# A two-layer fp32 decoder on one core: which engine makes the low halves of forty weight tiles

## The reference, cut to what matters

```python
def self_decoder_layer(x, mem, ...):
    proj = rmsnorm(x, norm_attn) @ w_in
    o_sb = stick_breaking_attention(...)
    o_mem = memory_branch(q_mem, mem, norm_mem, w_mem_kv)
    x = x + jnp.concatenate([o_sb.reshape(...), o_mem], axis=-1) @ w_out
    return x + conv_ffn(rmsnorm(x, norm_ffn), ffn_up, ffn_conv, ffn_down)
...
for g, (window, dilation) in enumerate(DIL_GROUPS):
    o_g, lse_g = dilated_window_attention(q_dil[:, :, hs], k_sh[:, :, hs], v_sh[:, :, hs], slopes[hs], window, dilation)
alpha = jax.nn.softmax(jnp.stack(lses, axis=0), axis=0)
```

## Time and profile before

| | |
|---|---|
| median of 3 runs | 1273.68 us (1272.54 to 1274.01) |
| profiled execution | 1273.02 us, of which the span from first to last instruction is 1271.2 |
| TensorE (PE) busy | 1217.4 us, 96% of the span |
| VectorE (DVE) busy | 800.3 us, 63% |
| ScalarE (ACT) busy | 553.7 us, 44% |
| GpSimd (POOL) busy | 102.6 us, 8% |
| granted TensorE clock, mean | 0.995 of full |

### The profile page before, as it was taken

The page is one execution under the profiler, slowest core; times in us unless marked ns, Lnnn a source line. Parts: engine busy times, 40 slices in busy tenths (PEclk is TensorE's granted clock), DMA queues, the critical chain, the costliest instruction groups (busy, mean ns, idle before and its releaser), DMA issues.

```text
span 1271.2 us, 16965 instructions
## 1 busy us (share of the span) xinstructions
PE 1217.4 (96%) x5975; PEld 999.4 (79%) x5975; DVE 800.3 (63%) x1243; ACT 553.7 (44%) x918; POOL 102.6 (8%) x133
## 2 busy tenths in 40 slices
PE   4889999989999999999999999889999999999998
PEld 3777888868788888878887877778788888888886
DVE  4956666664677777762247776776777777774226
ACT  4535666653444444441235553534544444442222
POOL 0301333333000000000002000000200000000000
PEclk9989999999999999999999999999999999999999
DMA  7411211203233333322251122121333333333552
GB/s 222 129 50 50 68 50 51 67 1 112 88 100 99 92 91 97 99 98 99 88 163 32 52 68 82 51 67 57 93 96 90 96 99 99 95 95 104 140 138 74
DMA packets 179796, 112.50 MB, mean 88 GB/s; under 512 B 20062, under 2 KB 171934, under 8 KB 179742
## 3 DMA queue, kind: packets, MB, share of 16 engines
q1 hardware_dynamic: 179742, 111.79, 29.6%
HBM read 107.58 MB, written 2.10 MB: 86 GB/s over the span
## 4 chain that ended last, share of the span: by engine, by line
PE 83%; DVE 10%; ACT 3%; issue 2%; DMA 1%; POOL 0%; DVEq 0%; SPq 0%; ACTq 0%; POOLq 0%
PE bank L1334 17%; PE bank L1336 17%; PE bank L1335 16%; PE bank L1614 8%; PE bank L1641 8%; DVE w_lo L881 2%; PE bank L1627 2%; PE bank L1561 2%; PE bank L1654 1%; DVE y_lo L887 1%; PE bank L1486 1%; PE bank L1488 1%; PE bank L1487 1%; PE bank L1539 1%; ACT w_hi L582 1%
## 5 line engine op out<-in xcount | busy, mean ns | idle before, releaser
L1334 PE MATMUL bank<-y_hi,w_hi 128*128 128x512 f32 x928 | 366.9, 395 | 3.7 <-DVE w_lo L881 2.6
L1336 PE MATMUL bank<-y_hi,w_lo 128*128 128x512 f32 x928 | 362.3, 390 | 0.0
L1335 PE MATMUL bank<-y_lo,w_hi 128*128 128x512 f32 x928 | 362.2, 390 | 0.0
L881 DVE TENSOR_TENSOR w_lo<-raw,w_hi 128x1024 fp32r<-128x1024 f32 x188 | 230.7, 1227 | 162.5 <-ACT w_hi L582 159.8
L582 ACT ACTIVATE w_hi<-raw 128x1024 fp32r<-128x1024 f32 x186 | 196.3, 1056 | 305.7 <-PE bank L1336 146.3
L1334 PEld LDWEIGHTS bank<-y_hi,w_hi 128*128 128x128 f32 x928 | 174.9, 188 | 43.0 <-issue 4.9
L1336 PEld LDWEIGHTS bank<-y_hi,w_lo 128*128 128x128 f32 x928 | 174.7, 188 | 37.0
L1335 PEld LDWEIGHTS bank<-y_lo,w_hi 128*128 128x128 f32 x928 | 175.0, 189 | 36.6 <-issue 1.2
L1614 PE MATMUL bank<-ar,w_hi 128*128 (+1 forms) x288 | 88.8, 390 | 0.8 <-DVE af L1099 0.8
L741 ACT ACTIVATE af<-af,conv 128x512 f32<-128x512 f32 x88 | 63.0, 716 | 37.0 <-DVE af L1099 37.0
L1641 PE MATMUL bank<-w_hi,ar 128*128 128x512 f32 x288 | 77.1, 390 | 0.8 <-DVE af L1099 0.8
(11 more groups left out here) (200 smaller groups left out, 1613.5 us busy)
## 6 DMA issues: line engine op xcount, KB each, us to landing
raw<-in_a_ffn_up SPq DMA_DIRECT2D x44, 512.0 KB, 3.7
raw<-in_b_ffn_up SPq DMA_DIRECT2D x44, 512.0 KB, 3.7
raw<-in_a_ffn_down SPq DMA_DIRECT2D x22, 512.0 KB, 3.2
raw<-in_b_ffn_down SPq DMA_DIRECT2D x22, 512.0 KB, 3.6
raw<-in_a_w_in SPq DMA_DIRECT2D x20, 512.0 KB, 3.8
raw<-in_w_kv_shared SPq DMA_DIRECT2D x12, 512.0 KB, 3.8
raw<-in_a_w_out SPq DMA_DIRECT2D x8, 512.0 KB, 3.7
raw<-in_b_w_in SPq DMA_DIRECT2D x8, 512.0 KB, 3.8
```

Of the source, the lines that this page charges most:

```text
L881: nc.vector.tensor_tensor(w_lo[:, m % SPLIT, :], raw[:, m % RAW, :], w_hi[:, m % SPLIT, :].bitcast(F32), ALU.subtract).then_inc(lo_done, 1)
L1334: mm(bank, w[0], y[0][:, k, :], start=(k == 0), stop=False)
L1335: mm(bank, w[0], y[1][:, k, :], start=False, stop=False)
L1336: last = mm(bank, w[1], y[0][:, k, :], start=False, stop=(k == KT - 1))
```

## The change

The low halves of forty tiles are made by GpSimd in place of VectorE: `POOL_LOW` holds the numbers 30 to 39 and 104 to 133. The instruction is the same tensor_tensor subtraction on 128x1024. GpSimd waits for `hi_done` and for `lo_done` of the tile before, so that the count stays in order. `squares` becomes `square(e, k)`, so that low halves can stand between the eight sums. In the output projection of layer A each of the eight low halves stands ahead of one sum, and two more (for the first pair of the up projection) follow; in layer B two stand ahead of the attention, 18 and then 8 follow the order of `SEQ_B`, and two come at the end. VectorE's `ring` returns for these tiles, without the wait for `hi_done`; ahead of the loop over the up projection's tiles VectorE waits until `lo_done` has reached the first tile that it makes again. GpSimd calls `ring` at some places for tiles that are not in `POOL_LOW`, and nothing happens there.

```diff
+        POOL_LOW = set(itertools.chain(range(N_OUTA + 2, N_UPA + 4), range(N_QMB + 2, N_UPB + 4)))
...
         @block.gpsimd
         def _(pool):
-            def squares(e):
...
+            def ring(n):
+
+                if n in POOL_LOW:
+                    pool.wait_ge(hi_done, n + 1)
+                    pool.wait_ge(lo_done, n)
+                    nc.gpsimd.tensor_tensor(w_lo[:, n % SPLIT, :], raw[:, n % RAW, :], w_hi[:, n % SPLIT, :].bitcast(F32),
+                                            ALU.subtract).then_inc(lo_done, 1)
+
+            def square(e, k):
...
-            squares(1)
-            squares(2)
-            squares(3)
+            for k in range(KT):
+                ring(N_OUTA + k + 2)
+                square(1, k)
+            ring(N_UPA + 2)
+            ring(N_UPA + 3)
+            for k in range(KT):
+                square(2, k)
+            ring(N_QMB + 2)
+            ring(N_QMB + 3)
+            for op, *a in SEQ_B:
+                if op == "P" and a[3] == KT:
+                    ring(nb(a[0], a[1]) + 2)
+                if op == "O":
+                    u, x = divmod(a[0], KT)
+                    if a[1] == OUT_KS_B[u][-1]:
+                        if x % 2:
+                            ring(N_OUTB + a[0] // 2 + 2)
+                        if u:
+                            square(3, x)
+            ring(N_UPB + 2)
+            ring(N_UPB + 3)
...
             def ring(n, m=None):
 
                 m = n if m is None else m
+                if isinstance(n, int):
+                    if n in POOL_LOW:
+                        return
+                    if n - 1 in POOL_LOW:
+                        dve.wait_ge(lo_done, n)
                 dve.wait_ge(hi_done, n + 1)
...
+                if n_up + 3 in POOL_LOW:
+                    dve.wait_ge(lo_done, n_up + 4)
                 with dve.Fori(0, 7) as i:
```

More of the change, by code:

```diff
@@ L11 @@
+import itertools
 from contextlib import ExitStack
@@ L511, in _ @@
         def _(pool):
-            def squares(e):
[L514 to L524, removed]
-                    else:
-                        ins = nc.gpsimd.tensor_tensor(ss[:], ss[:], sq[:, k % 2, :], ALU.add)
-                    ins.then_inc(ss_add, 1)
-            nc.gpsimd.memset(vv_gap.bitcast(F32), 0.0).then_inc(vv_zero, 1)
-            squares(0)
+            def ring(n):
[5 more added lines that the diff above has]
+            def square(e, k):
+                c = 8 * e + k
+                pool.wait_ge(sq_done, c + 1)
+                if c:
+                    pool.wait_ge(ss_add, c)
+                if k == 0:
+                    if e == 0:
+                        pool.wait_ge(tab_tr, 1)
+                    else:
+                        pool.wait_ge(ss_done, e)
+                    ins = nc.gpsimd.tensor_copy(ss[:], sq[:, 0, :])
+                else:
+                    ins = nc.gpsimd.tensor_tensor(ss[:], ss[:], sq[:, k % 2, :], ALU.add)
+                ins.then_inc(ss_add, 1)
+            nc.gpsimd.memset(vv_gap.bitcast(F32), 0.0).then_inc(vv_zero, 1)
+            for k in range(KT):
+                ring(k + 2)
+                square(0, k)
+            for n in range(N_QMA + 2, N_ATA + 5):
+                ring(n)
             added = 0
```

## The result

The changed kernel takes 1300.45 us in the median (1297.10 to 1304.07) against 1273.11 for the kernel before in the same runs: 1.0213 times as long, 95% interval 1.0193 to 1.0233, 27.3 us more. The prediction said 1287 with a range to 1296. The side was right, but the 13.3 us forecast are half of the 27.3 measured. The profiled execution took 1303.25 us, its span 1301.4.

The account below looks back on a forecast made before the run. The prediction took TensorE to bound the kernel, so only added TensorE waits count. Its eight terms summed to 13.3 us, taking the median from 1273.68 to 1287.0 us, with a range of 1277 to 1296.

Parts of the forecast that it names:

- the term: Start of the up projections: L898 and the eviction stand behind GpSimd's low half, +1.0 us in A and +1.0 in B.
- term 4: Attention, second score block: late softmax and tensor_scalar L1204 blocked by GpSimd, +2.3 us; 0.4 if not blocked.
- 5 first half: Coefficients of the first three heads: small chain behind a late qk_low, transposes behind a blocked L1247, +1.4 us.
- term 6: Attention tile at 806.01 whose low half TensorE itself already waits for, +1.2 us.
- term 7: Last score block: TensorE waits for qk_low, with ScalarE's w_hi late as well, +1.6 us.
- TensorE is the bound, so nothing gives a wait back: Whole kernel: the added TensorE waits count in full, 13.3 us in sum.
- term 3: Layer B's memory queries: L896 and the last qk_low stand behind GpSimd, making the memory scores late, +1.6 us.
- term 1: Layer A's output projection: the last square waits behind a low half and y_lo, +0.4 us, bounds 0 and 0.9.
- 5 (second half): Coefficients of the second three heads: multiplies L1230 caught in a hold, the eviction behind them late, +2.0 us.
- 8: Layer B's output projection: loop about 6.2 us where TensorE needs 5.4, last square after last y_lo, +0.8 us.
- The cascade rival: Each of the 18 attention tiles costs its 1.2 us, with other terms 26 us more, so 1300; chance 0.10.
- "Faster": GpSimd gets the port only when VectorE is idle, L898 runs as now: -4.2 us, 1269.5; chance 0.07.

Follow-up runs that it names:

- experiment 3: Changed kernel with the forty low halves back on VectorE, each released only after two GpSimd memsets: 1282.40 us against 1273.80 for the kernel before.
- experiment 1: Changed kernel with 8 groups of 7 to 13 dummy matmuls in long TensorE waits: 1292.97 us against 1273.80 for the kernel before.
- experiment 6: Kernel before with one added TensorE wait of five GpSimd memsets between two output tiles of layer A: 1280.35 us against 1274.22.
- experiment 9: Kernel before with only tile 123's low half made on GpSimd: 1278.48 us against 1272.74.
- experiment 4: Changed kernel with tiles 38, 39, 104, 105, 132 and 133 back on VectorE: 1297.07 us against 1273.80 for the kernel before.
- experiment 7: Changed kernel with tiles 104 to 109 back on VectorE: 1293.59 us against 1274.22 for the kernel before.
- experiment 5: Kernel before with one added TensorE wait of two GpSimd memsets between two output tiles of layer A: 1275.47 us against 1274.22.
- experiment 8: Kernel before with the halves of tiles 38, 104 and 132 made ahead of the rms chain: 1272.26 us against 1274.22.
- 10: Kernel before with 10 and 13 dummy matmuls in TensorE's two long waits at the start: 1270.89 us against 1272.74.
- 11: Kernel before with both the reordered halves of experiment 8 and the dummy matmuls at the start: 1268.75 us against 1272.74.
- four pieces: Changed kernel with each GpSimd low half cut into four subtractions of 256 columns: 1290.02 us against 1273.80 for the kernel before.

## Why the prediction was wrong in size

**Right: the exclusion and its numbers.** A moved tile takes 2.42 us (2.45 forecast). L898 stood at the up projections for 2.75 us, L896 2.48. TensorE's wait at the up projection's third tile is 2.11 (2.3 forecast); without the clock that stretch cost +0.9 in A and +1.0 in B, and 1.0 was the term. The tensor_scalar, for which I took the upper bound in term 4, does wait: L1204 took 2.05 us at 763.58, and TensorE then stood 2.25 us at 774.57 (2.3 forecast); the four of L1051 at 711.42 took 3.28 us. The Trainium skill (SBUF — State Buffer, "Who interferes with whom") says that a tensor_scalar in a 2-port mode fully blocks while GpSimd holds the ports, and that a two-input operation waits for a GpSimd operation that reads SBUF, not for one that only writes it. The traces at 763.58 and 711.42, and that of experiment 3 at 872.87, agree with the first; y_lo at 2.62 us behind a low half (at 931.40) and 0.74 us beside a memset agree with the second.

**Right in part by luck: the attention, 6.5 against 6.8.** Under 4, 5 first half, 6 and 7 the terms sum to 6.5 us of TensorE waits. Term 4 came as forecast and so did term 6 (1.02 us of wait became 2.20, +1.2), but term 7 was 0.75 instead of 1.6 (1.10 became 1.85), and over the whole stretch TensorE's idle time rose by only 2.8 us (6.5 to 9.3), as other waits shrank. The other 4.0 us are matmuls that lasted longer at the lower clock, which the sum did not have. The windows of this stretch, before and changed:

```profile
737.95:842.86 104.91, 98.42 (x666) 80.02 (x666) 74.17 (x221) 48.52 (x137) 0.00 (x0) 1.00 0.22 65
```
```profile
752.01:863.67 111.66, 102.37 (x665) 83.23 (x665) 71.08 (x208) 48.51 (x137) 31.15 (x13) 0.95 0.20 60
```

**The step that failed: "TensorE is the bound, so nothing gives a wait back".** The sum priced a TensorE wait at its own length and left the clock at nothing; it expected the durations of the matmuls unchanged, and TensorE was busy 18.8 us longer for as many of them. Behind most waits of about 2 us the chip granted the lower clock, for 3.4 or 6.8 us. The profiled pair lies 30 us apart, 16.8 more than the sum of 13.3. Of these 16.8 some 9 are the clock, by experiment 1, and 4.9 are term 3, the rest the other terms; experiment 6 shows the effect of a long wait alone and experiment 9 that of a single hold. It could be read beforehand. The windows of the kernel before, at its start, where the stretches follow waits of 2.67 and 3.30 us:

```profile
64.00:68.00 4.00, 4.00 (x12) 2.82 (x12) 1.74 (x3) 1.32 (x2) 0.00 (x0) 0.68 0.41 120
72.00:76.00 4.00, 1.59 (x7) 1.59 (x8) 2.31 (x3) 0.90 (x2) 0.00 (x0) 0.67 0.24 65
76.00:80.00 4.00, 4.00 (x14) 3.20 (x13) 1.29 (x2) 1.31 (x6) 0.00 (x0) 0.50 0.22 66
```

I had looked only at the windows where the change lay, and all of those said 1.00. The waits it had there were 1.0 to 1.8 us; my own terms added 0.5 to 2.2 to single ones, which brought them to the lengths seen here.

**Mis-sized: term 3, the queries and memory heads, +1.6 against 6.5** (without the clock). The chain's part came as forecast: the first memory scores of experiment 1 began 1.6 us later within that stretch. But the prediction put the tiles that follow at nothing, "as long as TensorE has its 24 matmuls queued", and did not look at the memory heads' scaled weights. Their scaling, L1014, begins 0.36 us after the start of a w_hi on ScalarE, both right behind the exponentials. Its fourth operation begins at about the time at which that w_hi is done and the hold starts, and GpSimd came in ahead of it (712.20). The lateness of the chain is not needed for this: scaling and w_hi stand to each other as before (0.36 us against 0.37), and in experiment 4, with the chain as before, the four took 3.28 us too. In experiment 1 this happened at three heads, and each head's transposes followed 1 to 2 us late. Experiment 7 gives the whole stretch back.

**Mis-sized: term 1, 0.4 against 1.3.** I looked at the last square and overlooked that TensorE already waited for the first of the moved tiles itself. The timeline of TensorE before:

```profile
284.98 0.50 PE L1486 MATMUL bank<-ar,w_hi 128*128 128x512 f32 x1 [1.78 <-DVE w_lo L881]
```

It is the case of term 6, +1.2, and at 2.95 us the clock added 2.7, which experiment 7 confirms: the same wait without the low clock lost 1.3.

**Terms 5 (second half) and 8, 2.8 against 4.1.** The hold in the coefficients did what was forecast (one tile: 2.1 us of wait, experiment 9). In the output projection every second y_lo took 2.62 us instead of 1.77, and the loop slowed by a little more than the 0.1 that I allowed. I did not measure the two apart.

**The rivals.** The cascade rival (1300, chance 0.10) has the right total by the wrong way: it charged lateness evenly, but tiles 104 to 109 cost 7 us and tile 123 alone over 5, and experiment 3 leaves at most 8.6 for all lateness. "Faster" falls with L935.

**Open.** Whether the clock falls behind a given wait differs between executions. Of 35 TensorE waits of 1.8 us or more behind 281 us in the traces kept here, 30 had 3.4 or 6.8 us of the lower clock behind them; five had none (1.81, 2.11, 2.25 twice, 2.96 us). Shorter ones had it at times: the 1.77 us wait of experiment 5 did, while the same wait before (1.78) did not, and so did the wait of 1.37 to 1.39 us ahead of layer B's output projection in experiments 5, 6, 8, 10 and 11. Executions of one kernel show it in their times. Of the 24 of the kernel before beside experiments 5 to 8, the six with a mean granted clock of 0.991 took 1275.5 to 1276.4 us, the six with 0.995 or 0.996 took 1270.9 to 1272.9; the four of the changed kernel have 0.979 to 0.986 and took 1304.1 to 1297.1. So the split between clock and waits holds to a few us. Why four pieces take 3.3 us rather than 2.9 is not settled either: VectorE's operations between them may be part of it.

## What to carry to other kernels

Before work goes from VectorE to GpSimd, list which operations of VectorE fall into the new operation's time; here every one with two SBUF inputs, even multiplies of 8 columns, and a tensor_scalar from SBUF to SBUF too, waited for the end of it. Then price each added TensorE wait by what it makes of the existing one: a wait that grew to about 2 us or more mostly had 3.4 or 6.8 us of half clock behind it as well, and about half of the time lost by that came back when the clock was kept up. Where TensorE must wait that long, a few dummy matmuls in the wait keep its clock up (experiments 1 and 10); moving the awaited operation into an idle gap ahead shortens the wait itself (experiment 8).

## What the runs showed of the hardware

A GpSimd memset (0.53 us for 128x512, output only) did not hold up VectorE operations with two SBUF inputs: y_lo kept 0.74 us at 896.74 in experiment 3, and four of L1147 that began inside a memset kept 0.75. It did hold up a tensor_scalar from SBUF to SBUF: 0.63 us instead of 0.28 at 872.87. GpSimd's tensor_tensor, which reads two tiles, held both (L935 2.75 us, L1204 2.05). A GpSimd operation that has asked gets its turn between two VectorE operations that follow each other within 0.03 us (332.09 to 332.55), so this chain of short dependent operations was broken at the first gap.
